# Which slots of the expert sum VectorE adds up, and which TensorE: 32 of 128 slots per tile before, 23 after

## The reference

```
s1, i1 = top_k(sc[:, :, 0], 16);  s2, i2 = top_k(sc[:, :, 1], 16)
top_s, ci = top_k(s1[..., :, None] + s2[..., None, :], 16)
e    = i1[ci // 16] * 128 + i2[ci % 16]          # 8 heads x 16 experts
gate = softmax(top_s)
act  = gelu(einsum('thkd,td->thk', u_tab[e], h))
out  = einsum('thk,thkd->td', gate * act, v_tab[e])
```

## Time and profile before

| what | value |
|---|---|
| median of three runs | 3440.44 us |
| profiled execution | 3432.67 us |
| its span, first to last instruction | 3430.9 us |
| PE busy (matmul) | 2841.4 us, 83% |
| VectorE busy | 2408.3 us, 70% |
| ACT busy | 1522.4 us, 44% |
| POOL busy | 1331.5 us, 39% |
| DMA | 1294.87 MB, 377 GB/s mean |
| gathers | 1140.92 MB, 81.9% of the 16 DMA engines' span |

### The profile page before, as it was taken

How to read it: one execution, slowest core, us unless ns; L and a number is a source line. 1 busy time by engine, 2 the same in 40 slices (tenths; PEclk the granted TensorE clock), 3 DMA queues, 4 the chain that set the end, 5 groups by cost and what they waited for, 6 DMA issues and landing times.

```text
span 3430.9 us, 31821 instructions
## 1 busy us (share of the span) xinstructions
PE 2841.4 (83%) x9166; PEld 1456.4 (42%) x9166; DVE 2408.3 (70%) x5603; ACT 1522.4 (44%) x4124; POOL 1331.5 (39%) x1097
## 2 busy tenths in 40 slices
PE   7988899986789788988898778977797888877677
PEld 5754455542445444543444333533353344433222
DVE  1258848794688658785889578966876587767954
ACT  2136334554346334643465345643563354333343
POOL 0023334452344434343444444444443434343432
PEclk8999999997999999999999999999998999888899
DMA  4269999998999999999999999999999999899998
GB/s 178 89 246 382 367 412 417 406 418 352 396 411 398 422 413 413 403 396 421 395 393 402 418 421 403 388 420 419 398 364 417 423 359 334 305 360 414 354 422 348
DMA packets 234342, 1294.87 MB, mean 377 GB/s; under 512 B 45700, under 2 KB 66084, under 8 KB 91446
## 3 DMA queue, kind: packets, MB, share of 16 engines
q0 software_dynamic: 156672, 1140.92, 81.9%
q1 hardware_dynamic: 77494, 151.92, 11.9%
HBM read 1275.74 MB, written 16.44 MB: 377 GB/s over the span
## 4 chain that ended last, share of the span: by engine, by line
PE 40%; DMA 27%; DVE 24%; ACT 4%; issue 4%; SPq 1%; POOL 0%; DVEq 0%; ACTq 0%
PE PS L992 17%; DMA R<-in_t_uv,idx 10%; DVE R L1623 9%; DMA wring<-in_w_out 6%; PE PS L699 5%; DMA wring<-in_w_query 5%; DMA R<-in_t_uv,idxS 4%; PE PS L938 3%; PE PS L965 3%; DVE xb L1634 3%; PE PS L665 2%; PE PS L780 2%; PE PS L779 2%; DVE SC L1586 2%; DVE SC L1583 2%
## 5 line engine op out<-in xcount | busy, mean ns | idle before, releaser
L632 POOL DMA_INDIRECT R<-in_t_uv,idx x1024 | 1266.2, 1237 | 1977.8 <-PE PS L992 1146.1
L992 PE MATMUL PS<-R,diag 128*128 128x512 f32 x3328 | 1660.8, 636 | 290.1 <-ACT diag L1252 242.1
L1623 DVE CUSTOM_DVE_ANT_0 R<-R,hb 128x1024 f32<-128x1024 f32 x1088 | 1316.6, 1221 | 575.1 <-DMA R<-in_t_uv,idx 490.5
L992 PEld LDWEIGHTS PS<-R,diag 128*128 128x128 f32 x3328 | 630.9, 201 | 1112.0 <-issue 586.9
L1243 ACT ACTIVATE acts<-dots 128x1 f32<-128x1 f32 x1088 | 218.9, 201 | 1264.2 <-DVE dots L1623 1244.9
L1634 DVE SCALAR_TENSOR_TENSOR xb<-R,wv,xb 128x1024 f32<-128x1024 f32 x256 | 328.3, 1282 | 2.8 <-ACT wv L1245 2.8
L1252 ACT ACTIVATE diag<-ident,wv 128x128 f32<-128x128 f32 x768 | 309.7, 403 | 38.3 <-PE PS L992 13.6
L699 PE MATMUL PS<-R 128*128 128x256 f32 (+1 forms) x1280 | 292.6, 384 | 38.0 <-ACT stg L1035 23.7
L1245 ACT ACTIVATE wv<-gate,acts 128x1 f32<-128x1 f32 x1024 | 303.5, 296 | 33.5
L699 PEld LDWEIGHTS PS<-R 128*128 128x128 f32 x1280 | 243.5, 197 | 104.7 <-issue 66.5
L938 PE MATMUL PS<-wring,T 128*128 128x512 f32 x256 | 147.7, 710 | 91.8 <-DMA wring<-in_w_out 91.6
(11 more groups left out here) (236 smaller groups left out, 2395.2 us busy)
## 6 DMA issues: line engine op xcount, KB each, us to landing
wring<-in_w_out SPq DMA_DIRECT2D x64, 512.0 KB
wring<-in_w_query SPq DMA_DIRECT2D x64, 512.0 KB
R<-in_t_win SPq DMA_DIRECT2D x27, 1024.0 KB, 18.6
R<-in_t_uv,idx POOLq DMA_INDIRECT x1024
prd<-stg SPq DMA_DIRECT2D x66, 128.0 KB
pr<-prd SPq DMA_DIRECT2D x8, 976.0 KB
xb<-in_x_prompt SPq DMA_DIRECT2D x8, 512.0 KB, 8.0
R<-in_w_out SPq DMA_DIRECT2D x8, 512.0 KB, 5.4
```

Of the source, the lines that this page charges most:

```text
L632: e.indirect_dma_start(dst, None, table, bass.IndirectOffsetOnAxis(ap=index, axis=0)).then_inc(S[s], c.count(name, s, 16))
L992: m = mm(bank(n), diag[:, NTH[s] % DR, :], pair(s)[:, D + 512 * n:D + 512 * n + 512], start=begins, stop=s == last_slot(t), skip_group_che ...
L1623: e.tensor_tensor_reduce(u, u, hb[:, tile_of(g) % 2, :], 1.0, 0.0, ALU.mult, ALU.add, dots[:, g % NW:g % NW + 1]).then_inc(dve_done, c.cou ...
```

## The change

The rule that picks VectorE slots is replaced. Of 128 slots of a prompt tile, VectorE had 5, 8, 11, ... 56 (every third, 18 slots) and 58, 63, ... 123 (every fifth, 14 slots): 32. It now has 2, then 6, 10, ... 58 (every fourth, 14 slots), then 66, 74, ... 122 (every eighth, 8 slots): 23. Over eight prompt tiles that is 256 before and 184 after. The sample tile has none in either.

```diff
 def on_dve(s):
-    r = s % P
-    return s < P * NTILE and (r % 3 == 2 if 3 <= r < 57 else 2 < r < P - 4 and r % 5 == 3)
+    return s < P * NTILE and s % (4 if 4 <= s % P < 60 else 8) == 2
```

## The result

| what | before | after |
|---|---|---|
| median, us | 3435.11 (16 runs, 3427.14 to 3451.62) | 3455.91 (16 runs, 3442.14 to 3469.24) |
| ratio, 95% interval | | 1.0061 (1.0047 to 1.0076) |
| profiled execution, us | 3432.67 | 3464.41 |
| span, us | 3430.9 | 3462.6 |
| PE busy, us | 2841.4 | 2937.3 |

The account below looks back on a forecast made before the run. DMA near 420 GB/s was taken to bound most slices, PE the attention and VectorE the searches; the terms 14.2 - 6.5 + 4 - 3 + 5 - 2.6 = +11 us on 3440.44 gave 3451 us, range 3428 to 3476 (the forecast's own 3443 to 3463).

Parts of the forecast that it names:

- A: Attention of the next tile, slots 1 to 32: two more slots on PE, 14.2 us slower over tiles 2 to 7.
- B: End of tile, slots 96 to 120, tiles 2 to 6: less VectorE work wins idle DMA time, -6.5 us.
- C: After the last weight product, slots 86 to 94, tiles 1 to 4: one more PE slot, +4 us.
- D: Tile 1, slots 14 to 54, top-16 search: three fewer VectorE slots, -3 us; slots 16 to 56 to show it.
- E: Sample tile's attention, slot 106 of tile 7 to slot 52 of tile 8: +5 us.
- F: Sample tile's top-16 search, slots 80 to 116 of tile 8: five VectorE slots instead of seven, -2.6 us.
- weight products: Slots 57 to 93: three more PE slots hidden, no cost; slots 56 to 96 stay at 119 us in middle tiles.
- C's own sign: What would show that term: slots 88 to 96 of tiles 2 to 4 take about 1 us more.
- Rival 2: Weight products become PE's, as added slots delay weight loads: 3475 us, chance 0.20; over 122 us would show it.
- Rival 1: VectorE is what counts and PE has room: -20 us, 3420 us, chance 0.16.
- rival 3: Nothing: transfers take back what attention loses, gains and losses cancel, 3440 us, chance 0.22.
- the diagonal wait: ACT's wait for a free diagonal buffer, 13.6 us before: no growth counted, at most the same again.

Follow-up runs that it names:

- x6: Kernel before, with VectorE taking every second slot from 5 to 23 in tiles 2 to 7 (ten instead of seven): 0.9993, -2 us.
- x5: Kernel before, with the new rule only in slots 0 to 32 of tiles 2 to 7 (eight VectorE slots instead of ten): 1.0027, +9 us.
- x1: Kernel before, with the new rule only in the first half of each tile (VectorE slots 2, 6, ..., 54): 1.0044, +15 us.
- x2: Kernel before, with the new rule only in the second half of each tile (VectorE slots 58, 66, ..., 122): 1.0030, +10 us.
- x7: Kernel before, with slot 113 of all tiles and tile 8's slots 98 to 118 moved from VectorE to PE: 0.9983, -6 us.
- x3: Kernel before, with the new rule in tiles 1 to 4 only: 1.0050, +17 us.
- x9: Kernel before, with the new rule in slots 33 to 56 alone (six VectorE slots instead of eight per tile): 1.0009, +3 us.
- x8: Kernel before, with more VectorE slots in slots 80 to 94 of tiles 1 to 4 and around the start of tile 8: 1.0012, +4 us.
- x10: Kernel after, with three diagonal buffers instead of four: 1.0050 against the kernel before.
- x11: Kernel before, with more VectorE slots in the attention, fewer in the searches, and slots 34 to 54 by fours: 0.9931, 3414.85 us, -24 us.

## Why the prediction was right in sign and half in size

One profile against one misleads here by several us a tile. Tile 1 took 401.0 us before and 405.5 after, but two kernels that leave tile 1 as it was are no quicker there. Tile 1 in x6:

```profile
218.00:624.60 406.60, 349.76 (x1167) 201.41 (x1168) 296.83 (x763) 184.38 (x513) 154.37 (x128) 0.93 0.97 392
```

And in x5:

```profile
217.00:625.40 408.40, 342.21 (x1168) 196.77 (x1169) 297.19 (x762) 184.12 (x513) 154.03 (x128) 0.95 0.97 390
```

So the terms are measured over all profiled kernels: for each stretch of each tile the time from the dot product of its first slot to that of the next stretch's, averaged over the kernels with the new rule there and in the two slots before (2 to 5), less the average over those with the old rule (5 to 10). Within such a group the times have a standard deviation of up to 3.0 us, mostly about 1.

| term | forecast | measured |
|---|---|---|
| A, attention, tiles 2 to 7 | +14.2 | +15.6 in slots 0 to 32, -6.4 in slots 33 to 56 |
| B, end of tiles 2 to 6 | -6.5 | +2.3 |
| C, slots 80 to 96, tiles 1 to 4 | +4 | +2.0 |
| D, tile 1, slots 0 to 56 | -3 | -1.7 |
| E, sample tile's attention | +5 | +3.9 in tile 7, +2.5 in tile 8 |
| F, sample tile's search | -2.6 | -2.0 |
| weight products, slots 57 to 79 | 0 | -2.4 |
| the rest (slots 80 to 96 of tiles 5 to 7, end of tile 1) | 0 | +0.2 |
| sum | +11 | +14, by the medians +21 (16 to 26) |

The measured terms sum to 14 us; with 40 differences of about 1 us uncertainty each, some 6 us together, that and 21 agree roughly, and 7 us have no place. By halves it is the same: the first half's terms give 10 us where x1 has 15 (9 to 21), the second's 4 where x2 has 10 (5 to 15). So the attention is shown as a cause by an experiment of its own (x5, 9 us); most of what the second half costs is not located.

- **B failed**, and it is the largest miss, 9 us. The prediction counted five multiply-adds against three over slots 96 to 120 and took their 2.56 us out of the stretch of slots 112 to 120, where DMA sat idle. But the multiply-add of a slot is issued two turns later: that of 113 falls in turn 115, of 118 in turn 120, and of 114 in turn 116. The stretch held one before and holds one after; the windows show 36 VectorE records in both. What VectorE was spared fell in slots 104 to 112, where transfers run at 413 GB/s before and 420 after [window above], and behind slot 120. Slots 104 to 112 and 120 to 128 of tile 6 before:

```profile
2394.90:2413.80 18.90, 15.63 (x40) 6.70 (x39) 18.53 (x58) 10.61 (x31) 11.77 (x9) 1.00 1.02 413
...
2435.60:2453.80 18.20, 16.39 (x56) 7.01 (x55) 13.61 (x28) 9.54 (x28) 11.17 (x10) 1.00 1.01 419
```

With three VectorE records fewer (55 for 58), slots 104 to 112 took longer and not less (19.4 us here; over tiles 2 to 6 and all kernels +3.9 us, why is open), slots 112 to 120 the same (+0.1), and slots 120 to 128 less (16.9 us here, with PE busy throughout; -2.0 over the five tiles). x7 took a multiply-add out of the right stretch and got 1.2 us of its length.

- **A** was right in mechanism, 5 us too high as a sum, and wrong in how it is spread: 15.6 - 6.4 = 9 us, which x5 gives too (+9, from 4 to 14). In tile 7 the first interval of heads fell by 0.23 us and not by 1.7, and the second grew by 0.98. The seven intervals together are 93.1 us; they were 92.3 before, and in the other kernels with the old slots there 91.7 three times (x2, x3, x9), 93.4 (x8) and 95.0 (x7). So a tile-7 head sequence costs at most 1.4 us more and not 3.4, and the old slots scatter by more than that; the prediction took the price of one interval between two others of the same kernel for that of every added slot. Tile 2, forecast at 1.2 for being near DMA's limit, took 5.3. And slots 33 to 56 returned 6.4 us that the prediction allowed only in part; by x5 and x9 they did so since the attention ran late, not for the multiply-adds taken from them.
- **C, D, E, F** came within 2 us each of their forecasts. In E's tile 7, slots 112 to 128 took 59.6 us for 54, and over all kernels slots 96 to 127 took 3.9 us more; but slots 112 to 128 took 58.6 us in x9 too, which has the old rule there, so how much of it is the change is not shown. C's own sign, slots 88 to 96 a microsecond longer, failed in tile 2 (23.4 us for 25.5), and D's, slots 16 to 56 of tile 1 shorter by 3 us, as well (126.7 for 126.0). F's stretch fell from 135 to 132.2 us as forecast.
- **The weight products** hid their three slots: 117.7 us where 119 was the mark and 122 the alarm. Rival 2 is out.
- **Rival 1** (PE has room) is out by x5 and by the sign of the result, and rival 3 (nothing) by the interval. The allowance of no growth for the diagonal wait was wrong in its number (51.6 us, where at most twice the 13.6 was allowed) and right in its price, as x10 shows.

## What to carry to other kernels

Before crediting an engine with work taken away, find the turn in which the instruction is really issued: with a lag of two turns, the saving here landed beside the stretch that could use it. Price a slot in both directions: in the attention of tiles 2 to 7, 12 slots more on PE cost 15.6 us in their own stretch (1.3 each, and 9 us after the next stretch had caught up), 18 slots fewer won some 12 us there (0.7 each). Test placement apart from count: the same 256 slots, spread evenly, cost 16 us, and placed by the engine that is full, near the same number (246 in x11) won 24.

## What was not expected of the hardware

- ACT waited 229.0 us instead of 51.6 for a free buffer and the kernel was no slower (1.0050 with three buffers, 1.0061 with four): this wait was only the shadow of a full PE.
- Stretches that no edit touched differ between profiled executions by some us: slots 0 to 32 of tile 1 took 107.0 us in the profile of before and 110 to 114 in others with the same rule there.
- The sample tile's attention ran at a granted clock of 0.81 in x8 and 0.88 or 0.89 in the kernels before, after and x11, and took 202.8 against 195, 197.6 and 188.7 us. What lowers it there is open.
